# One modulation chunk of the delta stage summed in the first two turns of the input product

## The chip, the cores and the metric

The kernel runs on one core of one Trainium2 chip. The metric is the device time of one execution in microseconds (us), the median of several runs. A separate execution was recorded by the hardware profiler, and all rows of the trace come from it.

## The reference, cut to what matters

Two transformer blocks of width 2048 over 256 tokens, all in float32. Each block begins with a modulation vector, made from one conditioning row `c`:

```
c_act = silu(c)
mod = c_act @ w_ada[l] + b_ada[l]                 # (2048) @ (2048 x 12288)
sh_m, sc_m, gt_m, sh_f, sc_f, gt_f = split(mod)   # six parts of 2048 columns
h = rmsnorm(x) * (1 + sc_m) + sh_m
proj = h @ w_in                                   # 2048 x 8208: the input product
o = [hgrn2(proj[:4096]), gated_delta(proj[4096:])]
y = o @ w_out
x = x + gt_m * rmsnorm(y);  h = rmsnorm(x) * (1 + sc_f) + sh_f;  x = x + gt_f * rmsnorm(ffn(h))
```

The second block has the same modulation and a mixer of several attentions. The change touches nothing but the time and place at which one 512-column piece of `mod` of the first block is computed.

## The kernel before, in words

**Modulation by chunks.** `mod` is cut into chunks of 512 columns (24 to a block). A chunk is a matrix-vector product over 2048 rows. Some chunks are computed by DVE: `Ada.step` (L243, and L239 for the first two) multiplies one 128x512 tile of `w_ada` by a column of `c_act` and adds it to one of two running sums, 16 steps a chunk; behind the last step one add (L248) joins the two sums; then PE sums over the partitions with four matmuls against ones (`sum_part`, L258). The tiles come in pairs, one DMA of 512 KB for two steps ("pair" 0 to 7 of a chunk), into a ring of buffers. `load_when_free` issues the load of a pair once the steps that used its buffer are done. Here a chunk of an `Ada` object is called its turn.

**The input product** (`phase_in_1`) multiplies the transposed h by `w_in`. It has 8 turns (1024 output columns each, in the order of `COLUMN_ORDER`) of 32 slots each, 256 slots. One slot is one half (512 columns) of one 128-row tile of the weights. For each slot ACT copies the weights rounded to fp32r (L1475, "high"), DVE subtracts to get the rest ("low", L1636), and PE multiplies: four matmuls high x high (L1309), then eight with the low parts (L1316, L1318). The split weights have four buffers, so ACT's slot s waits for PE to have done slot s-4. The whole is written as one program per engine, slot by slot; other work (the gate matmuls at slots 28 to 43, the HGRN2 levels, convolutions on POOL, evictions) is put behind fixed slots by `Pace`.

The weights come in groups of four slots (1 MB), through SP's queue (`refill`, L114), into a ring of two buffers (`RING = 2`). The refill of group g waits until DVE has split the last slot of group g-2, which is slot 4g-5. SP's queue is one program in order: behind each refill stand the loads of modulation pairs that `AFTER_REFILL` names, and a load that waits holds up the next refill.

In this stage two `Ada` objects run. `turn_ada` computes one chunk with its steps at slots 4 to 19 of turn 0, loads on POOL's queue, and its sum on PE behind slot 18; the last quarter of h needs it. `ada` computes chunks 8 to 14, one in each of the turns 1 to 7: step n stands behind slot 2 + 3n // 2 of the turn, so two slots in three, and its sum on PE behind slot 28 of the turn. It has two buffers (`IN_1_ASLOTS = 2`), in the place of the last columns' output.

**The delta stage** (`phase_gdn`) inverts a triangular system for 16 blocks by levels. In each of six levels (NI = 6) PE makes products for four quads (L1803), ACT copies them (L1774), and DVE writes masked results back (L1967, L1970). Each quad of each level is a point, 24 in all. Here a third `Ada` object computes chunks 15, 16 and 17: six of the 48 steps at the stage's front, the other 42 spread over the 24 points, with four buffers loaded by POOL. At the stage's end PE sums the chunks (L258) and runs 40 matmuls to keep busy (L541).

Of the kernel before, what the change touches and what calls it, by code (L numbers as in the profile page):

```python
# [18 lines left out]
KT = D // P  # L19
# [1105 lines left out]
            next(program, None)  # L1125


GDN_CHUNKS, FRONT_STEPS = (15, 16, 17), 6


AFTER_REFILL = {2: (2, 3), 3: (4,), 4: (5,), 5: (6, 7), 6: (8,), 7: (9,)}
X_HIGH_SLOTS = {0: (0,), 3: (1,), 6: (2,), 22: (3,)}
X_LOW_SLOTS = {0: (0,), 3: (1,), 8: (2,), 23: (3,)}
LEVEL_SLOT, LEVEL_SLOTS, TURN_STEP_SLOT = 78, 15, 4
# [3 lines left out]
def phase_in_1(nc, core, w_ada, w_in):  # L1138
# [32 lines left out]
    with ExitStack() as ctx:  # L1171
# [8 lines left out]
                       X[:].rearrange("p a b -> p (a b)").rearrange("p (s k n) -> p s k n", s=ASLOTS, k=AK),  # L1180
                       A[:, 0:HH, :, :].rearrange("p h c t -> p (h c t)")[:, 0:2 * CW].rearrange(
                           "p (c z n) -> p c z n", c=1, z=2))
        ada = Ada(ctx, nc, core, [(w_ada, 0, 2 * NT, 1)], LAST, IN_1_ASLOTS, ring)
        gate_work = A[0:HH, 0:2, :, :].rearrange("p h c t -> p (h c t)")
        b = hT[:, HH:2 * HH, :].rearrange("p a b -> p (a b)")
        block = ctx.enter_context(nc.Block())
# [9 lines left out]
        @block.sync  # L1196
        def _(sp):
            for g in range(RING, st.groups):
                i, q = g // st.unit, g % st.unit
                refill(sp, core, st, i, q)  # L1200
                for n in AFTER_REFILL.get(q, ()):
                    if 1 <= i + n // st.unit < st.turns:
                        ada.load_when_free(sp, i - 1 + n // st.unit, n % st.unit)
            prefetch(sp, core, core.streams["out_1"])

        @block.tensor
        def _(pe):
# [91 lines left out]
            for slot in range(SLOTS):  # L1299
                i, q, k = slot // TILES, slot % TILES // KG, slot % KG  # L1300
                c, row, part = place(k)
                kt = 2 * q + row
                if i == 0 and c == 0 and kt % 4 == 0:
                    pe.wait_ge(core.x_low, KT * x0 + kt + 4)
                pe.wait_ge(core.high_ready, slot + 1)
                for nt in range(NT):
                    if kt == 0 and nt % 2 == 0:
                        pe.wait_ge(core.free[c], i * NT + (f0[c] + nt + 2))
                    nc.tensor.matmul(acc(c, nt), w[:, k, 0, nt * P:(nt + 1) * P], x[:, kt, 0, :],  # L1309
                                     start=(kt == 0 and nt % 2 == 0), stop=False, skip_group_check=True)  # L1310
                if k < KG - 1:
                    pe.wait_ge(core.low_ready, (KG - 1) * (slot // KG) + k + 1)
                else:
                    pe.wait_ge(core.used, st.first + slot // KG + 1)
                for nt in range(NT):
                    nc.tensor.matmul(acc(c, nt), w[:, k, 0, nt * P:(nt + 1) * P], x[:, kt, 1, :], start=False,  # L1316
                                     stop=False, skip_group_check=True)
                    ins = nc.tensor.matmul(acc(c, nt), w[:, k, 1, nt * P:(nt + 1) * P], x[:, kt, 0, :], start=False,  # L1318
                                           stop=(kt == KT - 1 and nt % 2 == 1), skip_group_check=True)
                    if kt == KT - 1 and nt == 1:  # L1320
                        ins.then_inc(core.tile_ready, 1)
                ins.then_inc(core.parts_used, 1)
                pace.at(slot)
                if slot == TURN_SUM_SLOT:
                    turn_ada.sum_partitions(pe, 0)
                if i and slot % TILES == ADA_SUM_SLOT:
                    ada.sum_partitions(pe, i - 1)

        @block.gpsimd
        def _(pool):  # L1330
# [25 lines left out]
        def _(act):  # L1356
# [111 lines left out]
            for slot in range(SLOTS):  # L1468
# [10 lines left out]
                if i and slot % TILES in (0, 2):  # L1479
                    empty(i - 1, slot % TILES // 2)  # L1480
                pace.at(slot)
            act.wait_ge(core.ada_steps, KT * (ada.chunks0 + LAST))
            for c in range(2):
                empty(LAST, c)

# [1 line left out]
        def _(dve):  # L1487
# [140 lines left out]
                v.link(dve, ins)  # L1628

            pace = Pace([forget(), forget_gates(), diagonal()] + [level(l) for l in range(NL)] + [gated()])  # L1630
            step_slot = lambda n: 2 + 3 * n // 2
            for slot in range(SLOTS):
                i, k = slot // TILES, slot % KG
                g, part = slot // KG, place(k)[2]
                dve.wait_ge(core.high_ready, slot + 1)
                ins = nc.vector.tensor_tensor(w[:, k, 1, :], core.ring[:, g % RING, part, :],  # L1636
                                              w[:, k, 0, :].bitcast(F32), ALU.subtract)
                ins.then_inc(core.used if k == KG - 1 else core.low_ready, 1)
                for n in X_LOW_SLOTS.get(slot, ()):
                    low_x(n)  # L1640
                if slot == 3:
                    last_factors()
                    scale_input(nc, core, 2)
                if slot == 5:
                    scale_input(nc, core, 3)
                if TURN_STEP_SLOT <= slot < TURN_STEP_SLOT + KT:
                    turn_ada.step(dve, 0, slot - TURN_STEP_SLOT)
                if slot == TURN_SUM_SLOT + 3:
                    last_shift()
                for n in range(KT):  # L1650
                    if i and step_slot(n) == slot % TILES:
                        ada.step(dve, i - 1, n)
                pace.at(slot)
            ada.add_biases(dve)
    core.split_groups += st.groups
# [1449 lines left out]
```

## Time and profile before

| | us |
|---|---|
| median of 3 runs | 3023.97 |
| lowest and highest run | 3009.19, 3032.94 |
| the profiled execution | 3027.42 |
| its span in the trace | 3025.7 |
| granted TensorE clock, mean over the span | 0.968 |

Times in the trace are from the span's start. PE is the matrix engine, PEld its weight loads, DVE the vector engine, ACT the scalar engine, POOL GpSimd, SP the engine that only issues DMAs here. A row of the timeline has start, duration, engine, line of the kernel, operation, output<-inputs and count; in brackets the engine's idle time before it and what ended it. Instructions of one kind in a row are merged, so their duration is that of the run of them. Instructions overlap a little on each engine; the distance of two starts is the time that one costs. Behind "SPq" and "ACTq" stand issues of DMAs.

### The profile page before, as it was taken

The page shows a single profiled execution, that of the slowest core. Times are in us where ns is not written, and L with a number is a line of the kernel's source. Part 1 is how long each engine was busy: PE and PEld are TensorE (multiplying, and loading weights), DVE is VectorE, ACT ScalarE, POOL GpSimd, SP SyncE. Part 2 cuts the span into 40 slices and gives each one's busy share as a digit, 9 for nine tenths or more (in the row PEclk, how much of TensorE's full clock was granted, in tenths as well). Part 3 has the DMA queues.
Part 4 walks back from the last instruction along what each step waited for, and adds up shares of the span by engine and source line. Part 5 has one row for each costly group of instructions (what it writes and reads, how often), then busy time and mean ns, then how long its engine had stood idle before and what let it go on. Part 6 is the DMA issues. An engine that isn't in the chain of part 4 may idle for free. (4 is left out here: it accounts for less than half of the span.)

```text
span 3025.7 us, 55195 instructions
## 1 busy us (share of the span) xinstructions
PE 2878.1 (95%) x22459; PEld 2779.4 (92%) x22459; DVE 1923.7 (64%) x2679; ACT 1306.1 (43%) x2060; POOL 458.6 (15%) x575
## 2 busy tenths in 40 slices
PE   8799999998999999999999999998999999999998
PEld 8679998787999999999999889887989999999998
DVE  6657995785576666676676667676566644444554
ACT  1344446534354444444443444455443333333443
POOL 1002897110011111111110011121011000000000
PEclk6799999899999999999999999999999999999999
DMA  9657665633658787677774666575557755554544
GB/s 370 232 184 233 214 216 186 202 119 126 209 201 273 266 280 262 237 261 251 243 256 138 160 207 205 176 240 160 171 197 273 239 175 186 180 180 168 181 168 140
DMA packets 284224, 632.56 MB, mean 209 GB/s; under 512 B 24770, under 2 KB 45702, under 8 KB 283782
## 3 DMA queue, kind: packets, MB, share of 16 engines
q1 hardware_dynamic: 232400, 484.75, 47.7%
q0 software_dynamic: 40192, 142.63, 13.9%
q10 hardware_dynamic: 11446, 2.54, 0.6%
q8 instruction: 135, 2.21, 0.3%
q14 instruction: 51, 0.42, 0.0%
HBM read 627.77 MB, written 2.10 MB: 208 GB/s over the span
## 5 line engine op out<-in xcount | busy, mean ns | idle before, releaser
L1004 PE MATMUL accumulators<-h_parts,weight_parts 128*128 128x256 f32 x4672 | 1185.0, 285 | 16.8 <-DVE weight_parts L910 16.8
L1006 PE MATMUL accumulators<-h_parts,weight_parts 128*128 128x256 f32 x4672 | 1181.9, 285 | 0.0
L910 DVE TENSOR_TENSOR weight_parts<-weights,weight_parts 128x1024 fp32r<-128x1024 f32 x584 | 707.2, 1221 | 444.6 <-ACT weight_parts L836 443.8
L1004 PEld LDWEIGHTS accumulators<-h_parts,weight_parts 128*128 128x128 f32 x4672 | 905.0, 194 | 22.4 <-DVE weight_parts L910 22.3
L1006 PEld LDWEIGHTS accumulators<-h_parts,weight_parts 128*128 128x128 f32 x4672 | 905.5, 194 | 0.0
L836 ACT ACTIVATE weight_parts<-weights 128x1024 fp32r<-128x1024 f32 x584 | 600.7, 1054 | 649.0 <-PE accumulators L1006 296.1
L997 PE MATMUL accumulators<-h_parts,weight_parts 128*128 128x256 f32 x4672 | 763.1, 286 | 23.5 <-ACT weight_parts L836 13.6
L997 PEld LDWEIGHTS accumulators<-h_parts,weight_parts 128*128 128x128 f32 x4672 | 652.0, 194 | 28.8 <-ACT weight_parts L836 13.1
L1316 PE MATMUL accumulators<-in_h_parts,in_weight_parts 128*128 128x256 f32 x1024 | 262.0, 288 | 16.9 <-DVE in_weight_parts L1636 16.7
L1636 DVE TENSOR_TENSOR in_weight_parts<-weights,in_weight_parts 128x512 fp32r<-128x512 f32 x256 | 188.9, 749 | 110.6 <-ACT in_weight_parts L1475 110.3
L1318 PE MATMUL accumulators<-in_h_parts,in_weight_parts 128*128 128x256 f32 x1024 | 258.5, 284 | 0.0
L1475 ACT ACTIVATE in_weight_parts<-weights 128x512 fp32r<-128x512 f32 x256 | 152.9, 628 | 224.7 <-DMA weights<-in_w_in 122.9
L2490 PE MATMUL accumulators<-in_h_parts,in_weight_parts 128*128 128x256 f32 x1632 | 221.7, 291 | 11.4 <-DVE in_weight_parts L2869 5.1
L2490 PEld LDWEIGHTS accumulators<-in_h_parts,in_weight_parts 128*128 128x128 f32 x1632 | 207.2, 195 | 22.4 <-DVE in_weight_parts L2869 7.9
L1316 PEld LDWEIGHTS accumulators<-in_h_parts,in_weight_parts 128*128 128x128 f32 x1024 | 197.4, 193 | 23.1 <-DVE in_weight_parts L1636 22.7
L2625 ACT ACTIVATE in_weight_parts<-weights 128x512 fp32r<-128x512 f32 (+6 forms) x224 | 118.9, 553 | 184.0 <-PE accumulators L2490 124.9
L1318 PEld LDWEIGHTS accumulators<-in_h_parts,in_weight_parts 128*128 128x128 f32 x1024 | 197.9, 193 | 0.0
L908 DVE TENSOR_TENSOR h_parts<-wide,h_parts 128x512 fp32r<-128x512 f32 x108 | 74.4, 689 | 187.6 <-ACT weight_parts L836 187.5
L2869 DVE TENSOR_TENSOR in_weight_parts<-weights,in_weight_parts 128x512 fp32r<-128x512 f32 (+6 forms) x224 | 129.1, 593 | 92.7 <-ACT in_weight_parts L2625 91.8
L1309 PE MATMUL accumulators<-in_h_parts,in_weight_parts 128*128 128x256 f32 x1024 | 177.4, 296 | 7.2 <-DVE in_h_parts L1506 3.7
L243 DVE SCALAR_TENSOR_TENSOR ada_sums<-ada_weights,c_act,ada_sums 128x512 f32<-128x512 f32 x224 | 160.8, 746 | 25.2 <-DMA ada_weights<-in_w_ada 20.6
L835 ACT ACTIVATE h_parts<-wide 128x512 fp32r<-128x512 f32 x108 | 67.7, 627 | 238.4 <-DMA weights<-in_w_ff 129.9
(369 smaller groups left out, 2926.2 us busy)
## 6 DMA issues: line engine op xcount, KB each, us to landing
weights<-in_w_ff SPq DMA_DIRECT2D x128, 1024.0 KB, 6.6
weights<-in_w_in SPq DMA_DIRECT2D x80, 1024.0 KB, 6.2
h_t<-in_ada_w POOLq DMA_DIRECT2D x96, 512.0 KB, 5.7
weights<-in_ffn_w_gate SPq DMA_DIRECT2D x44, 1024.0 KB, 5.1
weights<-in_ffn_w_up SPq DMA_DIRECT2D x44, 1024.0 KB, 5.2
weights<-in_ffn_w_down SPq DMA_DIRECT2D x44, 1024.0 KB, 5.0
weights<-in_w_out SPq DMA_DIRECT2D x32, 1024.0 KB, 5.1
wide<-in_ada_w POOLq DMA_DIRECT2D x128, 256.0 KB, 3.9
```

Source lines behind the costliest of these rows:

```text
L243: ins = nc.vector.scalar_tensor_tensor(out=acc, in0=w, scalar=number, in1=acc, op0=ALU.mult, op1=ALU.add)
L836: nc.scalar.activation(w[:, held:held + take, 0, :], core.ring[:, q % RING, k:k + take, :], ACT.Copy).then_inc(core.high_ready, take)
L910: ins = nc.vector.tensor_tensor(w[:, held:held + take, 1, :], core.ring[:, q % RING, k:k + take, :], w[:, held:held + take, 0, :].bitcast( ...
L997: nc.tensor.matmul(accs[nt], w[:, held, 0, cols[nt]], xk[:, 0, :], start=(first and nt % 2 == 0), stop=False, skip_group_check=True)
L1004: nc.tensor.matmul(accs[nt], w[:, held, 0, cols[nt]], xk[:, 1, :], start=False, stop=False, skip_group_check=True)
L1006: ins = nc.tensor.matmul(accs[nt], w[:, held, 1, cols[nt]], xk[:, 0, :], start=False, stop=(last and nt % 2 == 1), skip_group_check=True)
L1309: nc.tensor.matmul(acc(c, nt), w[:, k, 0, nt * P:(nt + 1) * P], x[:, kt, 0, :], start=(kt == 0 and nt % 2 == 0), stop=False, skip_group_ch ...
L1316: nc.tensor.matmul(acc(c, nt), w[:, k, 0, nt * P:(nt + 1) * P], x[:, kt, 1, :], start=False, stop=False, skip_group_check=True)
L1318: ins = nc.tensor.matmul(acc(c, nt), w[:, k, 1, nt * P:(nt + 1) * P], x[:, kt, 0, :], start=False, stop=(kt == KT - 1 and nt % 2 == 1), sk ...
L1475: nc.scalar.activation(w[:, k, 0, :], core.ring[:, g % RING, part, :], ACT.Copy).then_inc(core.high_ready, 1)
L1636: ins = nc.vector.tensor_tensor(w[:, k, 1, :], core.ring[:, g % RING, part, :], w[:, k, 0, :].bitcast(F32), ALU.subtract)
L2490: ins = nc.tensor.matmul(out, stationary[:, a], moving[:, b], start=(kt == 0 and i == 0 and j == 0), stop=(kt == KT - 1 and i == 2 and j = ...
```

## The change

The chunk 15 goes from the delta stage to the input product. There `ada` has eight turns instead of seven, for chunks 8 to 15. Its turns 0 and 1 lie in the turns 0 and 1 of the product, with steps behind slots 22 to 37 and 42 to 60 (`step_slot`), and sums on PE behind slots 41 and 63 (`ADA_SUM_SLOTS`). Turns 2 to 7 keep the slots that they had. The loads of turns 0 and 1, and the first two of turn 2, stand in SP's queue behind the refills that `LOADS_OF_FIRST_TURNS` names: key g is the group, the pairs are (turn, pair). The delta stage computes chunks 16 and 17 alone; its front steps stay at six.

```diff
-GDN_CHUNKS, FRONT_STEPS = (15, 16, 17), 6
+GDN_CHUNKS, FRONT_STEPS = (16, 17), 6
...
 AFTER_REFILL = {2: (2, 3), 3: (4,), 4: (5,), 5: (6, 7), 6: (8,), 7: (9,)}
+LOADS_OF_FIRST_TURNS = {4: [(0, 0), (0, 1)], 7: [(0, 2)], 8: [(0, 3), (0, 4)], 9: [(0, 5), (0, 6)],
+                        10: [(0, 7), (1, 0)], 11: [(1, 1)], 12: [(1, 2)], 13: [(1, 3), (1, 4)], 14: [(1, 5)],
+                        15: [(1, 6), (1, 7)], 16: [(2, 0)], 17: [(2, 1)]}
+ADA_SUM_SLOTS = [41, 63]
...
-        ada = Ada(ctx, nc, core, [(w_ada, 0, 2 * NT, 1)], LAST, IN_1_ASLOTS, ring)
+        ada = Ada(ctx, nc, core, [(w_ada, 0, 2 * NT, 1)], st.turns, IN_1_ASLOTS, ring)
...
             for g in range(RING, st.groups):
                 i, q = g // st.unit, g % st.unit
                 refill(sp, core, st, i, q)
+                for turn, n in LOADS_OF_FIRST_TURNS.get(g, ()):
+                    ada.load_when_free(sp, turn, n)
                 for n in AFTER_REFILL.get(q, ()):
-                    if 1 <= i + n // st.unit < st.turns:
-                        ada.load_when_free(sp, i - 1 + n // st.unit, n % st.unit)
+                    if 2 <= i and i + n // st.unit < st.turns:
+                        ada.load_when_free(sp, i + n // st.unit, n % st.unit)
...
-                if i and slot % TILES == ADA_SUM_SLOT:
-                    ada.sum_partitions(pe, i - 1)
+                if slot in ADA_SUM_SLOTS:
+                    ada.sum_partitions(pe, ADA_SUM_SLOTS.index(slot))
+                if i >= len(ADA_SUM_SLOTS) and slot % TILES == ADA_SUM_SLOT:
+                    ada.sum_partitions(pe, i)
...
-            act.wait_ge(core.ada_steps, KT * (ada.chunks0 + LAST))
+            act.wait_ge(core.ada_steps, KT * (ada.chunks0 + st.turns))
...
-            step_slot = lambda n: 2 + 3 * n // 2
+            step_slot = lambda i, n: (22 + n, 42 + 5 * n // 4)[i] if i < 2 else TILES * i + 2 + 3 * n // 2
...
-                for n in range(KT):
-                    if i and step_slot(n) == slot % TILES:
-                        ada.step(dve, i - 1, n)
+                for turn in range(st.turns):
+                    for n in range(KT):
+                        if step_slot(turn, n) == slot:
+                            ada.step(dve, turn, n)
```

## Rows read from the trace of the kernel before

**Rows 1.** The page: busy time, share of the span and instructions of PE.
```profile
PE 2878.1 (95%) x22459; PEld 2779.4 (92%) x22459; DVE 1923.7 (64%) x2679; ACT 1306.1 (43%) x2060; POOL 458.6 (15%) x575
```

**Rows 2.** Windows, all engines: window, length, busy (count), granted clock, DMA share, GB/s.
```profile
99.10:582.10 483.00, 456.65 (x3560) 429.71 (x3560) 363.68 (x520) 240.74 (x393) 220.05 (x176) 0.99 0.65 210
582.10:720.60 138.50, 122.47 (x894) 109.61 (x894) 97.58 (x168) 47.13 (x73) 27.22 (x47) 0.89 0.30 92
```

**Rows 3.** Timeline of ACT, input product: splits of slots 26 and 43.
```profile
147.88 0.63 ACT L1475 ACTIVATE in_weight_parts<-weights 128x512 fp32r<-128x512 f32 x1 [0.81 <-PE accumulators L1318]
...
184.90 0.63 ACT L1475 ACTIVATE in_weight_parts<-weights 128x512 fp32r<-128x512 f32 x1 [1.95 <-PE accumulators L1318]
```

**Rows 4.** Line 243 in the input product: durations (ns), first and last start.
```profile
L243 DVE SCALAR_TENSOR_TENSOR ada_sums<-wide,c_act,ada_sums x98: 733/746/1252, 170.7 to 568.2; 128x512 f32<-128x512 f32 x98
```

**Rows 5.** Windows: sum over five levels of the delta stage, 612.3 to 676.13.
```profile
sum 63.83, PE 58.78 PEld 57.67 DVE 56.27 ACT 16.93 POOL 13.78; mean PE 11.76 PEld 11.53 DVE 11.25 ACT 3.39 POOL 2.76
```

**Rows 6.** Timeline of DVE: split of slot 15, step 13, split 18, step 15.
```profile
130.06 0.68 DVE L1636 TENSOR_TENSOR in_weight_parts<-weights,in_weight_parts 128x512 fp32r<-128x512 f32 x1
...
135.38 0.75 DVE L243 SCALAR_TENSOR_TENSOR attn_t<-scaled,c_act,attn_t 128x512 f32<-128x512 f32 x1
136.05 0.68 DVE L1636 TENSOR_TENSOR in_weight_parts<-weights,in_weight_parts 128x512 fp32r<-128x512 f32 x1
...
137.92 0.74 DVE L243 SCALAR_TENSOR_TENSOR attn_t<-scaled,c_act,attn_t 128x512 f32<-128x512 f32 x1
```

**Rows 7.** Timeline of PE and ACT at the end of the delta stage.
```profile
708.82 2.73 PE L258 MATMUL accumulators<-ones,ada_sums 128*128 128x1 f32 x24
...
720.87 1.06 ACT L822 ACTIVATE h_parts<-h_t 128x1024 fp32r<-128x1024 f32 x1 [6.82 <-PEq L1689]
```

**Rows 8.** DMA issues near 138.0, 138.4, 166.7 and 189.6: KB each, us to landing.
```profile
weights<-in_w_in SPq DMA_DIRECT2D x1, 1024.0 KB, 6.2
...
wide<-in_w_ada SPq DMA_DIRECT2D x1, 512.0 KB, 8.5
...
wide<-in_w_ada SPq DMA_DIRECT2D x1, 512.0 KB, 6.7
...
wide<-in_w_ada SPq DMA_DIRECT2D x1, 512.0 KB, 3.6
```

**Rows 9.** Timeline of SP's queue: refills of groups 2 to 6.
```profile
103.85 34.54 SPq L114 DMA_DIRECT2D weights<-in_w_in  x5
```

**Rows 10.** Timeline of ACT: splits of slots 20 to 22, shift of h's last quarter.
```profile
138.17 1.67 ACT L1475 ACTIVATE in_weight_parts<-weights 128x512 fp32r<-128x512 f32 x3 [3.13 <-DMA weights<-in_w_in]
140.73 1.71 ACT L319 ACTIVATE h_t<-h_t,modulation 128x256 f32<-128x256 f32 x4 [0.89 <-DVE modulation L176]
```

**Rows 11.** Timeline of PE: chunk sum, starts of slots 19 and 20.
```profile
139.44 1.05 PE L258 MATMUL accumulators<-ones,attn_t 128*128 128x1 f32 x8 [1.09 <-DVE attn_t L248]
140.36 1.13 PE L1309 MATMUL accumulators<-in_h_parts,in_weight_parts 128*128 128x256 f32 x4
...
143.00 1.02 PE L1309 MATMUL accumulators<-in_h_parts,in_weight_parts 128*128 128x256 f32 x4
```

**Rows 12.** Windows, all engines: the 3.5 us from 140; the clock is third from last.
```profile
140.00:143.50 3.50, 3.50 (x20) 3.50 (x20) 1.29 (x3) 2.68 (x6) 0.00 (x0) 0.56 0.95 304
```

**Rows 13.** Timeline of DVE: split of h's last quarter.
```profile
144.75 1.22 DVE L1506 TENSOR_TENSOR in_h_parts<-h_t,in_h_parts 128x1024 fp32r<-128x1024 f32 x1
```

**Rows 14.** Timeline of DVE, turn 1: splits of slots 49, 51-52, 56 and 61-63.
```profile
202.27 0.69 DVE L1636 TENSOR_TENSOR in_weight_parts<-weights,in_weight_parts 128x512 fp32r<-128x512 f32 x1 [3.05 <-ACT in_weight_parts L1475]
...
205.94 1.28 DVE L1636 TENSOR_TENSOR in_weight_parts<-weights,in_weight_parts 128x512 fp32r<-128x512 f32 x2
...
214.75 0.69 DVE L1636 TENSOR_TENSOR in_weight_parts<-weights,in_weight_parts 128x512 fp32r<-128x512 f32 x1 [1.45 <-ACT in_weight_parts L1475]
...
222.96 1.87 DVE L1636 TENSOR_TENSOR in_weight_parts<-weights,in_weight_parts 128x512 fp32r<-128x512 f32 x3
```

**Rows 15.** Timeline of PE, turn 1: low part of slot 57.
```profile
218.75 0.39 PE L1316 MATMUL accumulators<-in_h_parts,in_weight_parts 128*128 128x256 f32 x1 [1.55 <-DVE in_weight_parts L1636]
```

## The prediction

> **What bounds the kernel now.** The page comes first: PE is busy 95% of 3025.7 us [rows 1]. Then the two stages that the change touches, each as one window [rows 2]: the input product lasts 483.0 us with PE busy 456.65 and DVE 363.68, the delta stage 138.5 us with PE busy 122.47 and DVE 97.58. All else of the program is untouched.
>
> Third, the pace of the input product. Call slot n its n-th k-tile step, counted by the instructions of DVE's L1636, the first being slot 0. ACT splits slot s only once PE has left slot s-4, so the time between two of its splits is PE's pace: 0.63 + 0.81 = 1.44 us a slot, and 0.63 + 1.95 = 2.58 us in slots 28 to 43, where the gate matmuls ride along [rows 3]. DVE needs about 0.6 for its half of the split and 0.67 for a modulation step behind it, so 1.27. It keeps up as long as its step finds its weights, and in the kernel before it always does: no idle time of L243 stands in this stage [rows 4].
>
> Fourth, the delta stage: in its five levels from 612.3 to 676.13 PE is busy 58.78 of 63.83 us [rows 5]. DVE's steps are worth 5.05 us there and no more.
>
> **The change, delta stage.** 16 steps, one closing add, eight POOL loads and four sum matmuls go. Steps fall from 42 to 26 over 24 points, so from seven a level to four or five. (a) In the five levels the gain is at most PE's idle 5.05 us. DVE's busy time there falls from 56.27 [rows 5] by 14 steps of 0.67 to 46.9, well under PE's 58.78, so I take all of it: -5.05. (b) The last level ends with DVE alone; its points carry 1, 1, 1, 2 steps instead of 1, 2, 2, 2: 2 x 0.67 = -1.34, a step being 136.05 - 135.38 = 0.67 [rows 6]. (c) At the stage's end PE sums three chunks in 2.73 us ahead of its warming matmuls, and the next stage's ACT had waited 6.82 us for PE's end [rows 7]; two chunks take 1.82: -0.91. The POOL loads gone are worth nothing: DVE waits for none of them in the levels. Sum -7.3, bounds -2.25 (PE's own work fills the levels anyway) and -10.8 (16 x 0.67, were DVE alone the bound).
>
> **The change, input product.** Turn 0 now takes 16 steps at slots 22 to 37, turn 1 at 42 to 60; turns 2 to 7 keep their slots. What moves is not DVE's work (there is room: a slot is 1.44 or 2.58) but SP's queue, which carries the 1 MB refills and the 0.5 MB step loads in program order, and the reach ahead of a load. Only two buffers of two steps each exist. Before, a pair of rows was loaded about five slots ahead of its step; now a load stands behind the refill of group g, issued when slot 4g-5 is done, and its step comes one to three slots later.
>
> Landing times: a step load alone takes 3.6 us, one issued right behind a refill 6.7 [rows 8], so 7.1 from the refill's issue with some 0.4 for SP to issue each. I take 7.1, as this is the row that the new order repeats; the bounds are 3.6 and the 8.5 of the first such load [rows 8].
>
> (d) *Refill 5.* Before, SP issued refills 2 to 6 in one run [rows 9], the one of group 5 once slot 15 was done at 130.06 + 0.68 = 130.7. Now two step loads stand before it. The first waits for step 13 of the chunk in turn 0, the second for step 15, which ends at 137.92 + 0.74 = 138.7 [rows 6]. SP stands until then; refill 5 goes out at 139.15, 8.4 us later, and refill 6 is queued behind it. It lands 6.2 us later (the row of refill 6, which had company too [rows 8]), at 145.35. ACT split slot 20 at 138.17 [rows 10]; now it ends its split at 146.0. PE began slot 20 at 143.00 [rows 11] and now begins at 146.0: +3.0. Behind a wait of 1.09 us and the sum matmuls PE took 2.64 us for slot 19 (140.36 to 143.00) [rows 11], at a granted clock of 0.56 [rows 12], which is mostly 1.2 instead of 2.4 GHz. After 3 us idle I charge slot 20 the same 2.64 instead of the 1.80 it had: +0.8. The Trainium skill (TensorE: Matmul & The Clock Gate, "Part 1: The HAM clock gate") calls half rate the state after idleness; by that rule each stall of some us below would cost a slow slot more, by 1.2 us each; I leave this to the slower rival. The last quarter of x (ACT from 140.73 [rows 10], DVE's 1.22 us at 144.75 [rows 13], 5.2 us from first to last) begins behind slot 22, at 147.2, and is ready at 152.4, before PE's slot 24 at 153.0. Term: +3.8.
>
> (e) *Slot 26.* Refill 7 goes out behind slot 23 at 151.4; pair 2 lands 7.1 later at 158.5. DVE reaches that step at 156.05, so slot 27's split is done at 158.5 + 0.67 + 0.6 = 159.8, and PE wanted it at 157.8: +2.0. (f) *Slot 28.* Refill 8 goes out at 159.8 and pair 3, needed one slot later, lands at 166.9. Slot 29 is split at 168.2; PE, which adds 1.14 us of gate matmuls from slot 28 on, wanted it at 163.9: +4.3. (g) *Slots 32 and 36* repeat it, but a group takes PE 4 x 2.58 = 10.3 there and DVE 7.1 + 3 x 1.27 = 10.9: +0.6 twice, +1.2. (h) *Turn 1.* Pairs 5 and 6 stand behind refills 14 and 15, three and two slots ahead of slots 54 and 57. From slot 51's split (done at 206.55) to slot 61's (223.6) DVE took 17.0 us before, 1.45 of it idle [rows 14]. Now it has eight steps in there instead of four (+2.7), loses the idle time (-1.5) and waits twice for 7.1 - 3.1 = 4.0: 26.2 us. PE ran slot 57 from 218.75 on [rows 15] and would reach slot 61's low part at 225.4, 18.85 us after the mark, so the term is 26.2 - 18.85, taken as +7.3. Pair 3 stands behind refill 13, two slots ahead of slot 49, and costs nothing: ACT's logarithm behind slot 48 already holds DVE up there, with 3.05 us of idle before slot 49's split [rows 14]; with that cover gone it would be some 4 us. (i) One more sum of a chunk stands in PE's stream: 2.73 / 3 = +0.9 [rows 7].
>
> Sum of d to i: 3.8 + 2.0 + 4.3 + 1.2 + 7.3 + 0.9 = +19.5. The loss is not given back, since turns 2 to 7 follow slot by slot. With -7.3 the net is +12.2 us. The profiled execution took 3027.42 us around its span of 3025.7, 3.45 above the median of 3023.97 shown; the forecast is 3039.6 on its footing and 3036 on the median's.
>
> **Rivals.** *Loads covered.* If a step load lands 3.6 us from its own issue whatever stands before it, and DVE's three slots of lead cover the rest, d to h vanish but for the odd tenth: 0.9 - 7.3 = -6.4, 3018. For it: each of the 98 steps found its weights before. Against it: the 6.7 of a load behind a refill, and leads of one to three slots where five were. The Trainium skill (DMA: Bandwidth & Descriptors, "Two DMAs through the same engine are not ordered") says that transfers on one queue may finish writing out of order, which would allow 3.6; the row with 6.7 does not bear it out, as the load came in just behind the refill. Chance 0.2.
>
> *Slower.* The wait sits in SP's queue from slot 20 to 61, at seven places. If a load behind a refill needs 8.9 us from the refill's issue (8.5 from its own, the first one's row), each wait is 1.8 longer: +12.6, and PE then stands for 2 us or more before slots 29, 33, 37, 55 and 58, each paid with one slow slot as slot 19 was: 5 x 1.2 = +6. Together 12.2 + 18.6 = +31, 3055. It decides from about 8.9 us on (at 8.0 the sum would be some +19, inside 1%). For it: two loads often follow one refill. Against: later ones had 6.7. Chance 0.12.
>
> *The delta stage gives only 2.25*, as PE fills its levels either way: +17, 3041. Speaking for it: PE's 92% in the levels. Against: PE does stand idle 5.05 us there [rows 5], and its products wait for DVE's results alone. Chance 0.08.
>
> **How the numbers follow.** The forecast has the remaining 0.6. A measurement of this kernel tells 1%, 30 us, from no change. Faster by that would need more than the whole delta gain: 0.02. Slower: the second rival, 0.11 with some of its cases just inside. Same: 0.87. The range reaches from the covered case less the scatter of the runs (3009 was seen), 3010, to the slower case, 3055.
>
> **What would show it.** SP's refill of group 5 about 8 us after slot 15; ACT at slot 20 near 145 to 147; idle of DVE's L243 put down to the load of w_ada, some 6 us each at slots 28, 32 and 36 and 4 at 54 and 57; PE's L1316 waiting for DVE near slots 29, 55 and 58. The input product near 502 us and the delta stage near 131. No idle before L243 would prove me wrong and the first rival right; a delta stage of 136 the third.

## The result and the profile after

| | before | changed |
|---|---|---|
| median of the comparison, us | 3020.46 | 3040.86 |
| span of the profiled execution, us | 3025.7 | 3045.7 |
| granted TensorE clock, mean of the span | 0.968 | 0.966 |

The ratio is 1.0067, 95% interval [1.0052, 1.0082]: 20.4 us slower by the medians, inside 1%. Executions at a low granted clock (here one of 4841 us at 0.71) are not in the ratios. The forecast was +12.2 us with a range from 3010 to 3055: the sign was right, the time lies in the range, and the size was 8 us short.

The page of the changed kernel, busy time of each engine (compare [rows 1]):

```profile
PE 2881.0 (95%) x22459; PEld 2781.9 (91%) x22459; DVE 1922.2 (63%) x2679; ACT 1306.5 (43%) x2060; POOL 452.6 (15%) x567
```

PE's busy time grew by 2.9 us and the span by 20.0, so on balance nearly all of it is waiting. The instructions fell by eight on POOL alone (the loads moved to SP); PE and DVE have as many as before. In the changed kernel's rows the lines of the input product have other numbers: ACT's split is L1483 (L1475 before), DVE's L1644 (L1636), and PE's matmuls are L1315 and L1322 (L1309 and L1316). To see where PE waits, cut both kernels at the same three instructions: DVE's split of slot 0, PE's first matmul with `pick` in the delta stage, and the next stage's first ACT of L822. The windows of the two stages (the columns are those of [rows 2]), before:

```profile
99.78:582.19 482.41, 456.65 (x3561) 429.75 (x3561) 363.69 (x521) 240.12 (x393) 219.49 (x177) 0.99 0.65 210
582.19:720.87 138.68, 122.47 (x894) 109.58 (x894) 97.57 (x168) 47.10 (x74) 27.19 (x47) 0.89 0.30 92
```

and after:

```profile
100.15:611.28 511.13, 463.11 (x3568) 434.60 (x3569) 373.05 (x538) 240.19 (x393) 218.64 (x177) 0.97 0.64 207
611.28:740.50 129.22, 117.76 (x886) 107.03 (x886) 86.78 (x150) 47.03 (x73) 21.57 (x39) 0.91 0.21 66
```

The delta stage gave 9.5 us, the input product lost 28.7, and 28.7 - 9.5 = 19.2 is nearly all of the 20.0 in the span. The prediction had the product near 502 and the delta stage near 131, so the product was missed by 9 us and the delta stage, the other way, by 2. Within the product PE's time outside its busy 463.11 grew from 25.8 to 48.0, +22.3, and its busy time by 6.5, of which some 0.9 is the added sum and the rest comes with a clock of 0.97 instead of 0.99. What follows the two stages took 2304.8 us before and 2305.2 after.

**What DVE waits for.** Line 243 in the input product and the delta stage's front (the counterpart of [rows 4], where no such wait stood):

```profile
L243 DVE SCALAR_TENSOR_TENSOR ada_sums<-wide,c_act,ada_sums x112: 733/747/1227, 156.8 to 597.3; 128x512 f32<-128x512 f32 x112
...
  DMA wide<-in_w_ada: 39.4, 10
```

Ten waits, 39.4 us, each for a load of step weights. The timeline of DVE has them one by one; four of its rows are those of slots 28, 32 and 36 and, last, one that waits for something else:

```profile
171.91 0.75 DVE L243 SCALAR_TENSOR_TENSOR ada_sums<-wide,c_act,ada_sums 128x512 f32<-128x512 f32 x1 [7.44 <-DMA wide<-in_w_ada]
...
183.80 0.75 DVE L243 SCALAR_TENSOR_TENSOR ada_sums<-wide,c_act,ada_sums 128x512 f32<-128x512 f32 x1 [6.75 <-DMA wide<-in_w_ada]
...
195.69 0.75 DVE L243 SCALAR_TENSOR_TENSOR ada_sums<-wide,c_act,ada_sums 128x512 f32<-128x512 f32 x1 [6.75 <-DMA wide<-in_w_ada]
...
210.62 0.49 DVE L239 TENSOR_SCALAR ada_sums<-wide,c_act 128x512 f32<-128x512 f32 x1 [8.33 <-PE accumulators L258]
```

**SP's queue** around refill 5, the counterpart of [rows 9]:

```profile
104.23 22.33 SPq L114 DMA_DIRECT2D weights<-in_w_in  x3
137.90 2.90 SPq L201 DMA_DIRECT2D wide<-in_w_ada  x2
140.84 14.29 SPq L114 DMA_DIRECT2D weights<-in_w_in  x3
```

The run of five refills is now one of three, two step loads at 137.90, and refill 5 at 140.84, although its buffer was free at about 131. ACT and PE then stand at slot 20 ([rows 10] and [rows 11] before):

```profile
148.58 1.67 ACT L1483 ACTIVATE in_weight_parts<-weights 128x512 fp32r<-128x512 f32 x3 [11.79 <-DMA weights<-in_w_in]
```
```profile
149.26 1.22 PE L1315 MATMUL accumulators<-in_h_parts,in_weight_parts 128*128 128x256 f32 x4 [5.49 <-ACT in_weight_parts L1483]
```

What PE waited for between 141 and 262 us, by the view of waits (total us, times, longest), which held 1.6 and 0.9 us from 141 to 232 before:

```profile
PE accumulators L1322 <- DVE in_weight_parts L1644: 18.9, 8, 5.8
PE accumulators L1315 <- ACT in_weight_parts L1483: 5.5, 1, 5.5
```

**Slot by slot.** How much later DVE splits a slot than before, each counted from its own slot 0 (the start of that split in the timeline, after minus before; so worked out):

| slot | 19 | 26 | 29 | 42 | 49 | 58 | 64 | 76 | 106 | 126 | 255 |
|---|---|---|---|---|---|---|---|---|---|---|---|
| changed kernel, us late | 1.4 | 9.8 | 19.3 | 18.2 | 19.9 | 30.1 | 31.3 | 33.7 | 32.0 | 28.2 | 28.7 |

All of the loss is there by slot 76. Some 4 us come back between slots 106 and 126, and then it stays. The 1.4 us at slot 19 are scatter: PE has them at slot 17 already, before the first load that the change adds goes out at 137.90, and the other kernels have -1.4 to 1.0 at slot 19.

### The profile page after: what moved, and what is told of

Read it like the earlier page. It is cut to its first block and busy times, and to the rows that moved or that the text cites. A ratio compares the mean times of both kernels' runs of the same rounds, so it can differ in the third digit from the quotient of the medians.

```text
span 3045.7 us, 55196 instructions
## 1 busy us (share of the span) xinstructions
PE 2881.0 (95%) x22459; PEld 2781.9 (91%) x22459; DVE 1922.2 (63%) x2679; ACT 1306.5 (43%) x2060; POOL 452.6 (15%) x567
## 5 line engine op out<-in xcount | busy, mean ns | idle before, releaser
L1322 PE MATMUL accumulators<-in_h_parts,in_weight_parts 128*128 128x256 f32 x1024 | 265.3, 291 | 33.9 <-DVE in_weight_parts L1644 33.8
L1483 ACT ACTIVATE in_weight_parts<-weights 128x512 fp32r<-128x512 f32 x256 | 152.6, 627 | 252.5 <-DMA weights<-in_w_in 148.6
L1644 DVE TENSOR_TENSOR in_weight_parts<-weights,in_weight_parts 128x512 fp32r<-128x512 f32 x256 | 186.1, 740 | 81.6 <-ACT in_weight_parts L1483 81.2
L1322 PEld LDWEIGHTS accumulators<-in_h_parts,in_weight_parts 128*128 128x128 f32 x1024 | 199.6, 195 | 41.2 <-DVE in_weight_parts L1644 40.5
L1315 PE MATMUL accumulators<-in_h_parts,in_weight_parts 128*128 128x256 f32 x1024 | 178.0, 297 | 12.6 <-ACT in_weight_parts L1483 8.9
L243 DVE SCALAR_TENSOR_TENSOR ada_sums<-ada_weights,c_act,ada_sums 128x512 f32<-128x512 f32 x210 | 151.5, 746 | 25.5 <-DMA ada_weights<-in_w_ada 21.4
## 6 DMA issues: line engine op xcount, KB each, us to landing
h_t<-in_ada_w POOLq DMA_DIRECT2D x96, 512.0 KB, 5.9
wide<-in_w_ada SPq DMA_DIRECT2D x64, 512.0 KB, 5.4
```

Source lines behind the costliest of these rows:

```text
L243: ins = nc.vector.scalar_tensor_tensor(out=acc, in0=w, scalar=number, in1=acc, op0=ALU.mult, op1=ALU.add)
L1483: nc.scalar.activation(w[:, k, 0, :], core.ring[:, g % RING, part, :], ACT.Copy).then_inc(core.high_ready, 1)
```

## The experiments

Each kernel stands beside runs of the kernel before on the same chip; the last was timed once. The product and delta lengths come from one profiled execution each, cut at the three instructions above. How far they scatter is seen in two kernels whose input product is that of before: 480.1 and 481.6 against 482.4 us. So a difference of 2 us in one stage length tells nothing. What follows the two stages, where no kernel differs, took 2289 to 2306 us in the eleven profiled executions, so the total of one execution tells less than its stages.

| kernel | product, us | delta, us | ratio to before, 95% interval |
|---|---|---|---|
| before | 482.4 | 138.7 | |
| changed | 511.1 | 129.2 | 1.0067 [1.0052, 1.0082] |
| e4_delta_only | 480.1 | 128.7 | 0.9950 [0.9930, 0.9970] |
| e5_product_only | 512.0 | 138.5 | 1.0097 [1.0068, 1.0126] |
| e2_order | 504.8 | 129.2 | 1.0036 [1.0016, 1.0057] |
| e1_sum38 | 509.0 | 128.7 | 1.0063 [1.0041, 1.0085] |
| e3_early | 492.1 | 130.4 | 0.9992 [0.9978, 1.0006] |
| e8_pool4 | 486.3 | 130.1 | 0.9984 [0.9967, 1.0001] |
| e6_all | 485.8 | 130.3 | 0.9982 [0.9963, 1.0000] |
| e7_pace | 480.7 | 128.7 | 0.9971 [0.9948, 0.9995] |
| e9_one_chunk | 481.6 | 127.0 | |

### The two halves alone

e4_delta_only is the kernel before with a delta stage of two chunks; chunk 15 is computed nowhere, its columns being copied from chunk 14.

```diff
-GDN_CHUNKS, FRONT_STEPS = (15, 16, 17), 6
+GDN_CHUNKS, FRONT_STEPS = (16, 17), 6
...
+            nc.vector.tensor_copy(core.mod[:, 0, 60:64], core.mod[:, 0, 56:60])
```

> The kernel before with the delta stage computing chunks 16 and 17 alone; chunk 15 is computed nowhere (its four columns of the modulation are a copy of chunk 14's), so 4 MB of loads and 16 steps are left out of the program. What the delta half of the change is worth. My reading of the changed kernel's trace: the delta stage goes from 138.7 to about 129.2 us, nothing else moves, the kernel is 9 to 10 us faster than before (ratio 0.997). The rival that the stage is held by PE all along, with the 9.5 us of the trace due to something else (for instance a better phase of the clock): 2 to 3 us. The rival that the later stages give the gain back: the stage shorter, the total unchanged.

Measured: a delta stage of 128.7 us, 9.9 under before, with an untouched product at 480.1. The whole is 0.9950 [0.9930, 0.9970], 9 to 21 us; the stage's gain lies at the low end of that, and the rest does not come from the two stages: behind the two stages this profiled execution was 11.9 us shorter than before (2293.0 against 2304.8), and those of e3_early and e8_pool4 by 13 to 16.

e5_product_only is the changed kernel with the old delta stage, so that chunk 15 is computed twice.

```diff
-GDN_CHUNKS, FRONT_STEPS = (16, 17), 6
+GDN_CHUNKS, FRONT_STEPS = (15, 16, 17), 6
```

> The changed kernel with the delta stage as it was: chunk 15 is computed twice, in the input product and in the delta stage. If the parts add, the product stays at 511 us (28.7 over the kernel before), the delta stage is back at 138.7 (9.5 over the changed kernel), and the whole is 25 to 33 above the kernel before, a ratio near 1.0095. If the delta stage's gain were bound to something else (its order of points or loads), the stage would stay near 130 and the ratio near 1.0067. If the loss in the product were partly given back in the delta stage (work that is only shifted), the whole would be well under 20 above.

Measured: 512.0 and 138.5 us, ratio 1.0097, 29 us above before. Each stage has the length that its own edit gives it, whatever the other does. The loss is the product's alone, and the gain the delta stage's.

### Refill 5 behind the step loads

```diff
-LOADS_OF_FIRST_TURNS = {4: [(0, 0), (0, 1)], 7: [(0, 2)], ...
+LOADS_OF_FIRST_TURNS = {5: [(0, 0)], 6: [(0, 1)], 7: [(0, 2)], ...
```

> The changed kernel with the two step loads behind refill 4 put behind refills 5 and 6. Theory Q (a load that waits in SP's queue holds the refills behind it): refill 5 goes out at about 131 us, as in the kernel before, slot 20 is split some 8 us sooner, PE's 5.5 us before slot 20 go, and the input product is 4 to 7 us shorter than the 511.1 of the changed kernel, so 504 to 507; the whole about 5 below the changed kernel. Rival L (the step loads themselves are what is late, whatever stands behind them): the first step then has its weights no sooner than before or later, and the product stays at 509 to 513. In both the waits of DVE's steps at slots 28, 32 and 36 stay near 7 us each.

Measured: the product is 504.8 us, 6.3 shorter; DVE's lateness at slot 26 is 1.4 us instead of 9.8. SP's queue issues refills 2 to 5 in one run again:

```profile
104.84 27.50 SPq L114 DMA_DIRECT2D weights<-in_w_in  x4
137.87 0.37 SPq L201 DMA_DIRECT2D wide<-in_w_ada  x1
139.74 0.37 SPq L114 DMA_DIRECT2D weights<-in_w_in  x1
```

and PE's wait for ACT at slot 20 is gone (141 to 256 us):

```profile
PE accumulators L1322 <- DVE in_weight_parts L1644: 18.4, 7, 5.9
```

Its waits for DVE are as they were, and so are DVE's for its loads, 40.5 us in 11. Two separate losses, then: what a waiting load holds up behind it, and the load's own lateness. The rival by which only the loads' own lateness counts is refuted.

### The sum behind slot 41

The row at 210.62 waits for PE's sum of chunk 8: the first step of the next chunk (behind slot 42) writes the running sum that PE reads, and PE reads it behind slot 41, having lagged up to four slots. This kernel sums behind slot 38, the first slot after the last step.

```diff
-ADA_SUM_SLOTS = [41, 63]
+ADA_SUM_SLOTS = [38, 63]
```

> The changed kernel with the sum of the first chunk behind slot 38 of PE's program instead of slot 41. In the changed kernel's trace DVE stands 8.33 us before the first step of turn 1 (slot 42), until PE has done that sum. Theory L (the lead lost there is what makes the loads and refills of turn 1 late): the wait shrinks to under 2 us, refill 12 goes out some 6 us earlier, PE's waits for DVE in slots 50 to 61 (12 us) fall to some 6, and the input product is 4 to 7 us shorter. Theory Q (each load behind its refill costs its landing time, whatever the lead): the wait at slot 42 goes, the waits of 4 to 5 us at slots 54 and 57 stay, as they are counted from slots 51 and 55, and the product is 0 to 2 us shorter. The waits in turn 0 stay in both.

Measured: the 8.33 us before that step shrink to 0.59, and the waits at slots 54 and 57 stay (4.26 and 4.76 us), as theory Q had it. The product is 509.0 us, 2.2 shorter, and the ratio 1.0063 is not told apart from the changed kernel's 1.0067. At slot 64 DVE is 28.5 us late instead of 31.3, but 1.0 of that difference stands already at slot 19; from slot 42 to 64 the lateness grows by 11.2 us here and by 13.1 there. So the wait was worth some 2 us of the product at most, no more than the scatter. DVE's lead over PE covered the rest: PE's timeline has no idle of its own there.

### Every load one refill earlier

```diff
-... 7: [(0, 2)], 8: [(0, 3), (0, 4)], 9: [(0, 5), (0, 6)], 10: [(0, 7), (1, 0)], 11: [(1, 1)], 12: [(1, 2)], ...
+... 7: [(0, 2), (0, 3)], 8: [(0, 4), (0, 5)], 9: [(0, 6), (0, 7)], 10: [(1, 0), (1, 1)], 12: [(1, 2), (1, 3)], ...
```

> The changed kernel with each step load of turns 0 and 1 one place or so earlier in SP's program: pairs 2 and 3 behind refill 7, 4 and 5 behind 8, 6 and 7 behind 9, the first two of turn 1 behind 10, then 12: (2, 3), 13: (4, 5), 14: 6, 15: 7 and the next turn's first, 16: its second. The two loads ahead of refill 5 stay where they are. Theory Q (order in the queue): the waits of DVE at slots 28, 32 and 36 (7.4, 6.8, 6.8 us) become waits of 2 to 4 us at slots 30 and 34, PE's 5.8 us before slot 29 goes, and the product is 7 to 12 us shorter. Theory B (two buffers are too few for a step in each slot, in any order): the waits only move to other slots, their sum of 39 us falls by less than a quarter and the product by less than 3 us. The 5.5 us of PE before slot 20 stay in both.

Measured: 492.1 us, 19.0 shorter, more than any theory gave it, and the whole level with before, 0.9992 [0.9978, 1.0006]. DVE's waits for its loads:

```profile
  DMA wide<-in_w_ada: 15.3, 6
```

From pair 2 on the loads stand three or five slots ahead of use in turn 0 and four to nine in turn 1; in the changed kernel it is one to three and two to seven. Waits of 2.64, 4.87 and 4.07 us are left at slots 26, 30 and 34, whose pairs have three slots, longer than the 2 to 4 us that theory Q gave. The theory that two buffers are too few in any order is refuted. The wait at slot 20 stayed in this kernel (ACT had 12.19 us of idle there), since its first two loads still stood behind refill 4.

### Four buffers and POOL's queue

The turns 0 and 1 get an `Ada` object of their own with four buffers, loaded by POOL, sums behind slots 39 and 63.

```diff
+        early = Ada(ctx, nc, core, [(w_ada, 0, 2 * NT, 1)], 2, ASLOTS,
+                    flat(HI, 2 * HH).rearrange("p (s k n) -> p s k n", s=ASLOTS, k=AK))
...
+            for n in range(2 * AGROUPS):
+                early.load_when_free(pool, n // AGROUPS, n % AGROUPS)
```

> The changed kernel with chunks 8 and 9 (turns 0 and 1) computed by an object of their own that has four buffers in rows of the wide tile that are still free, loaded through POOL's queue; SP's queue carries no step loads before turn 2, and the sum of the first stands behind slot 39. All of the change's work is done, with the same steps in the same slots. Theory Q: DVE finds nearly every pair landed, PE's waits before slots 20, 29 and 50 to 61 go, the product is 20 to 28 us shorter than the changed kernel's and within 4 us of the one before; the whole is 5 to 9 us faster than the kernel before. Theory C (more bytes in the first turns slow the refills, whatever the queue): the product stays 8 us or more above the one before, with ACT waiting longer for refills. Theory W (16 steps more are too much for DVE in the first two turns): DVE has no idle time left in slots 44 to 61 and the product stays 5 us or more above.

Measured: DVE waits 1.4 us for its loads, once, and the product is 486.3 us, 24.8 shorter and 3.9 above before. Loads issued far ahead now travel beside the refills, and ACT waits longer for these (from 141 to 262 us; 32.4 us in seven waits in the changed kernel):

```profile
ACT in_weight_parts L1483 <- DMA weights<-in_w_in: 42.1, 11, 6.9
```

But up to slot 58 this costs nothing: DVE is 0.8 us early there. At slot 64 it is 8.2 us late, and SP's queue shows why:

```profile
209.20 0.37 SPq L114 DMA_DIRECT2D weights<-in_w_in  x1
220.93 0.37 SPq L201 DMA_DIRECT2D wide<-in_w_ada  x1
221.34 0.47 SPq L114 DMA_DIRECT2D weights<-in_w_in  x1
```

The load at 220.93 is the first of turn 2. It still stands behind refill 14 and waits until all but two of the 32 steps of turns 0 and 1 are done, which the step behind slot 58 completes at 220.9. Refill 15, whose buffer was free at 215.8, waits behind it, and PE stands at slot 60:

```profile
228.16 1.23 PE L1313 MATMUL accumulators<-in_h_parts,in_weight_parts 128*128 128x256 f32 x4 [4.12 <-ACT in_weight_parts L1483]
```

So what is lost behind slot 58 comes once more from a load that waits ahead of a refill, and not from the traffic; this kernel with that load further back was not tried. In ratio, 0.9984, this is the same as the reordered kernel on SP's queue below, for twice the buffers.

### All three edits, and steps with room between them

e6_all has the order of e3_early, the first loads of e2_order and the sum of e1_sum38.

> The changed kernel with three edits: the first two step loads behind refills 5 and 6, every later load one refill earlier, and the first sum behind slot 38 instead of 41. Adding the single effects (refill 5 no longer held, some 5 us; earlier loads 19.0; the earlier sum about 2) gives a product of 511.1 - 26 = 485, 3 over the kernel before, and with the delta stage's -9.5 a total 6 to 8 us below the kernel before, ratio 0.9975 to 0.998. If the effects overlap because two loads behind one refill still land 5 us apart, the product stays near 490 and the total is level with the kernel before (0.999 to 1.000). If two buffers cannot hold enough, the product stays above 495.

Measured: 485.8 us where the single effects gave 485; within the scatter they add. e7_pace spreads the steps of turn 0 as those of turn 1 are spread. Three more things change with it: turn 1 starts behind slot 44, the first sum stands behind slot 40, and some loads of turns 1 and 2 stand behind other refills:

```diff
-LOADS_OF_FIRST_TURNS = {... 10: [(1, 0), (1, 1)], 12: [(1, 2), (1, 3)], 13: [(1, 4), (1, 5)], 14: [(1, 6)],
-                        15: [(1, 7), (2, 0)], 16: [(2, 1)]}
+LOADS_OF_FIRST_TURNS = {... 10: [(1, 0)], 11: [(1, 1)], 12: [(1, 2), (1, 3)], 13: [(1, 4)], 14: [(1, 5), (1, 6)],
+                        15: [(1, 7)], 16: [(2, 0), (2, 1)]}
...
-            step_slot = lambda i, n: (22 + n, 42 + 5 * n // 4)[i] ...
+            step_slot = lambda i, n: (22 + 5 * n // 4, 44 + 5 * n // 4)[i] ...
...
-ADA_SUM_SLOTS = [38, 63]
+ADA_SUM_SLOTS = [40, 63]
```

> As the kernel with all three edits, but the steps of turn 0 stand four to every five slots (behind slots 22 to 40) instead of one to every slot, those of turn 1 behind slots 44 to 62, and the sums behind slots 40 and 63. If the density of the steps matters (a group of four slots has two loads of 512 KB beside its 1 MB refill), the product is 2 to 5 us shorter than with the steps in every slot, so 481 to 484, and the total some 10 below the kernel before (0.9965). If only the order of the loads matters, the product equals that of the other kernel within 1.5 us. If the waits come from the step's distance to the end of its turn, it is longer by 1 to 3.

Measured: 480.7 us, level with before's product within the scatter, with 16 more steps in it. Its windows:

```profile
100.27:580.93 480.66, 456.98 (x3569) 429.41 (x3569) 376.06 (x539) 240.03 (x393) 214.60 (x177) 0.99 0.67 220
580.93:709.68 128.75, 119.17 (x886) 108.05 (x886) 86.89 (x150) 47.11 (x74) 21.37 (x39) 0.89 0.21 66
```

DVE's busy time is 376.06 against 363.69 before, and no cost of that is seen; the clock is back at 0.99. PE waited for DVE and ACT from 141 to 232 us:

```profile
PE accumulators L1322 <- DVE in_weight_parts L1644: 2.3, 3, 0.8
PE accumulators L1315 <- ACT in_weight_parts L1483: 0.4, 1, 0.4
```

This version is the only one with the whole work that is faster than before by more than its interval: a median of 3011.70 us against 3020.92, ratio 0.9971 [0.9948, 0.9995]. Against e6_all its stage is 5.1 us shorter, at the upper end of what the density of steps was expected to give; the ratios of the two do not tell them apart. Nor is density shown as the cause: each pair now has at least four slots ahead of use where some in e6_all have three, and the longest of DVE's waits in turn 0 fell from 4.95 to 2.68 us.

### What is left in the delta stage

e9_one_chunk is e4_delta_only with chunk 16 left out as well, its columns copied in the same way.

```diff
-GDN_CHUNKS, FRONT_STEPS = (16, 17), 6
+GDN_CHUNKS, FRONT_STEPS = (17,), 6
```

> The kernel before with chunks 15 and 16 left out (their columns are copied from chunk 14), so that the delta stage computes chunk 17 alone and the input product is as it was. Theory P (with two chunks PE already runs the five levels without a gap, 57.44 us busy of 57.52): the five levels stay within 0.5 of the 57.5 us they have with two chunks; only the last level (4.69 us), where DVE works alone, loses some 0.7 to 1.3 and the closing sums 0.9, so the stage goes from 128.7 to some 127. Rival D (the levels wait for DVE's steps in proportion to their number): the stage loses another 8 to 10 us, to some 120. In both the input product is 480 to 483.

Measured: the stage is 127.0 us. Five levels, from the first masked copy of the first level to that of the last, as windows in the kernel before, the changed one and this one:

```profile
613.54:677.33 63.79, 58.74 (x514) 57.63 (x514) 56.73 (x84) 16.55 (x23) 14.51 (x23) 1.00 0.44 133
```
```profile
641.42:698.94 57.52, 57.44 (x514) 57.25 (x514) 47.52 (x68) 16.55 (x23) 8.36 (x15) 1.00 0.28 83
```
```profile
613.10:670.27 57.17, 57.17 (x514) 57.17 (x514) 39.77 (x55) 16.53 (x23) 2.10 (x7) 1.00 0.04 11
```

PE has 514 matmuls in each. With three chunks they take 63.79 us, with two 57.52 and with one 57.17: from two chunks on PE is the whole bound, and leaving another chunk out took 1.7 us off the stage (against e4_delta_only), no more than its scatter among the kernels with two chunks (128.7 to 130.4).

## Why the prediction was right and where it fell short

**(a) Five levels: -5.05 forecast, -6.3 measured** (63.79 to 57.52). The rule used was right (DVE's steps are worth what PE stands idle and no more), and e9_one_chunk shows PE as the bound. The size was off because the 58.78 us in [rows 5] were taken as PE's floor. The same 514 matmuls are busy 58.74 in one and 57.44 in the other: so the busy time, modelled from overlapping records, seems to hold some waiting too.

**(b) The last level: -1.34 forecast, -1.7 measured** (from the first to the last masked copy 6.42 and 4.69 us). **(c) One sum fewer: -0.91 forecast, -0.90 measured**, ACT's idle before L822 being 6.82 in [rows 7] and 5.92 after. That leaves 0.6 of the stage's 9.5 with no term, less than the scatter. The rival in which the stage gives only 2.25 is refuted by all eight kernels with two chunks, whose stage took 128.7 to 130.4 us.

**(d) Refill 5: +3.8 forecast, +6.7 measured.** The mechanism is as told: a wait in SP's queue, the refill 9.7 us late, then PE without weights. PE's start of slot 24 comes 15.47 us after that of slot 19 (142.09 to 157.56), where it took 8.76 (140.36 to 149.12); undoing it gave 6.3. Two things were mis-sized. The refill landed after 7.7 us, not 6.2:

```profile
weights<-in_w_in SPq DMA_DIRECT2D x1, 1024.0 KB, 7.7
wide<-in_w_ada SPq DMA_DIRECT2D x1, 512.0 KB, 3.9
```

Refill 6 went out right behind it, and both step loads ahead of it were still under way; that this company made it slower is likely but was not tried. And the clock charged one cold slot at +0.8; there were two. PE's slots 20 and 21 took 2.72 and 2.56 us instead of 1.80 and 1.44, at a granted clock of 0.51 in the window of the 6 us behind the wait (the third from last column):

```profile
149.00:155.00 6.00, 5.74 (x27) 5.74 (x28) 3.32 (x7) 5.26 (x11) 0.00 (x0) 0.51 0.09 35
```

**(e) to (g) Slots 26 to 37: +7.5 forecast, some +10 measured** (16.8 of lateness from slot 19 to 42, less the 6.7 by which e2_order differs there). The places are those named: 2.46 us at slot 26 and 7.44, 6.75 and 6.75 at slots 28, 32 and 36, where "some 6 us" stood. The landing was too short. From 160 to 262 us a single load right behind a refill took 6.8 to 7.0 us from its own issue in four cases, 8.4 in one and 9.4 in another; where two stood behind it, the first took 8.2 in one case and 7.4 to 7.6 in three, and the two together had a median of 7.7 to 7.9 in these three. The waits of DVE at slots 28, 32 and 36 ended 8.7, 8.0 and 8.0 us after the refill's issue, where 7.1 had been taken. Three of the answers on DMA issues, from 163.6, 176.2 and 230.0 us:

```profile
wide<-in_w_ada SPq DMA_DIRECT2D x1, 512.0 KB, 8.2
...
wide<-in_w_ada SPq DMA_DIRECT2D x2, 512.0 KB, 7.9
...
wide<-in_w_ada SPq DMA_DIRECT2D x1, 512.0 KB, 6.9
```

The forecast took 6.7 for all from [rows 8], a row in which the load had the queue behind the refill to itself. Behind slot 28 PE stood 5.77 us, and resumed at half clock for the next 5:

```profile
173.30:178.30 5.00, 4.99 (x17) 3.33 (x18) 3.75 (x6) 1.84 (x5) 0.00 (x0) 0.50 0.24 54
```

This is the lower of the two levels, 1.2 GHz. So the slower rival was right in its two mechanisms (a landing slower than 7.1, a slow stretch behind a long wait) and wrong in their number: slots 33 and 37 cost PE 0.5 us of waiting together, and behind the turn 1 waits of 5.03 and 3.33 us the clock was 0.72 (from 240.60 to 246.00) and 0.66 (from 249.90 to 254.90), so the low level held for a part only. The rival's own sum for a landing of 8.0 us, some +19, came out almost to the number, and that is luck: it holds no slow slots, and it charges two waits that PE hardly had. The Trainium skill (TensorE: Matmul & The Clock Gate, "Part 1: The HAM clock gate") has TensorE at half rate after it was idle; the trace agrees behind the waits of 5.49 and 5.77 us, with granted clocks of 0.51 and 0.50, and in part behind that of 5.03 us, with 0.72. The forecast had set that rule aside for all stalls but one, and of the 5.6 us by which PE's work itself got longer it had charged 0.8.

**(h), (i) Turn 1 and the added sum: +8.2 forecast, +13.1 measured** (lateness 18.2 at slot 42, 31.3 at slot 64). The forecast waits of 4.0 at slots 54 and 57 came as 4.28 and 4.69. Three it had not: pair 3 at slot 49, priced at nothing under ACT's logarithm, waited 2.61 us; the pair of slot 47 waited 2.19; and the first step of the turn stood 8.33 us behind PE's sum, of which some 2 us at most reached the product. That last one was left out altogether: the added sums were priced as matmuls in PE's stream, and who waits for them was not asked. For the pair of slot 49 the forecast had named some 4 us if its cover were gone; a part of them came, as PE stood 2.10 and 0.71 us at slots 50 and 51.

**The sum.** The terms of the product, by lateness, are 1.4 us of scatter up to slot 19, 6.7 for (d), 10.1 for (e) to (g), 13.1 for (h) and (i), 2.4 from slot 64 to 76 that the forecast had nothing for, and 5.0 given back: 28.7. The mechanism of the forecast held, and each of its three groups was sized too small.

**"The loss is not given back."** Nearly so: of 33.7 us at slot 76, 28.7 stand at the end. Between slots 106 and 126 some 2.3 to 3.8 us come back in all eight kernels with the added chunk, whatever their lateness. They are a loss of the kernel before that the others have less of. Before, ACT waits 6.28 us for a refill at 301.67 and PE then stands at slot 109,

```profile
306.85 0.38 PE L1316 MATMUL accumulators<-in_h_parts,in_weight_parts 128*128 128x256 f32 x1 [1.79 <-DVE in_weight_parts L1636]
```

with a granted clock of 0.66 in the five us from 307; in the changed kernel ACT's wait is 3.52 us at 331.25, PE has no wait at that slot, and the clock is 1.00 from 328.5 to 372.5. Why that refill has more room was not tried.

**Loads covered**, the rival with 0.2, is refuted by ten waits. It leaned on the rule of the Trainium skill (DMA: Bandwidth & Descriptors, "Two DMAs through the same engine are not ordered") by which a later transfer may finish its writing before an earlier one has. Nothing here shows that: in this stretch each load landed after the refill it stood behind (refill issued at 163.23 and landed after 6.5, the load issued at 163.64 and landed after 8.2).

## What to carry to other kernels

A load with a wait in a queue that also carries the main stream's refills holds up all behind it: put it behind the refill whose turn comes when its buffer is free, not by when its data are wanted, and then give it room ahead of use (four to nine slots in the kernel that lost nothing; three left waits of 2.6 to 4.9 us). Before moving work into an engine's spare time, list the transfers it brings, how many stand behind one another, and the first instruction that must wait for its closing step; here 16 steps cost 28.7 us in one order and nothing measurable in another, with the steps a little further apart. A stall of 5 us on PE can be paid twice, once as the wait and once in the clock behind it: 0.51 and 0.50 behind two of them, 0.72 behind a third.

## What the runs showed that was not expected

- PE's busy time for the same 514 matmuls was 58.74, 57.44 and 57.17 us at a granted clock of 1.00, so it is no floor.
- The first of two 512 KB loads behind a 1 MB refill landed 7.4 to 8.2 us after its issue, a single one mostly after 6.9, and the two that went out ahead of refill 5 after 3.8 and 3.9.
- With four buffers on POOL's queue the first 58 slots had no loss left; the 8 us behind them came from one load on SP's queue that waited ahead of refill 15.
- Slot 19, which PE took at a clock of 0.56 in 2.64 us before [rows 11, 12], took 1.7 us after, though it again followed 1.08 us of idle and the same eight matmuls. The stretch from 143 to 149, in which PE did next to nothing, shows a granted clock of 0.92, and the 6 us behind it 0.51: the clock fell at some time in the wait, and rose again only while PE worked.
